# A cap on how far weight splitting runs ahead of the latent queries, and a later place for the squares of the queries' heads

## What is computed

```python
q  = (rms_norm(q_lat, q_a_gain) @ w_q_b).reshape(B, S, 8, 192)      # latent queries, 8 heads of 128 + 64 (rope)
kv = (rms_norm(kv_lat, kv_a_gain) @ w_kv_b).reshape(B, S, 8, 256)
q, k = rms_norm(q, q_gain), rms_norm(k, k_gain)                     # per head: needs the sum of squares of each head
q = concat([q[..., :128], rope(q[..., 128:], positions)])
p = softmax(q @ k.T * 192 ** -0.5)                                  # causal
o_mla = p @ v
mixed = concat([rms_norm(o_mla, g1), rms_norm(o_swa, g2)])
h = x + mixed @ w_out
```

## Time and profile before

| | |
|---|---|
| median of 3 runs | 3234.4 us (3231.15 to 3234.57) |
| the profiled execution: its own time | 3236.4 us |
| its span in the trace | 3234.6 us |
| TensorE (PE) busy | 99% |
| VectorE (DVE) busy | 65% |
| ScalarE (ACT) busy | 47% |
| mean DMA rate | 204 GB/s |
| weight splits: DVE L2140, ACT L1908 | 1101 each, 1223 and 1058 ns |

### The profile page before, as it was taken

One profiled execution on the slowest core, in us unless ns is written; L12 is line 12 of the kernel. 1 busy time (PEld: TensorE's weight loads), 2 busy tenths in 40 slices (PEclk: granted clock), 3 DMA queues, 4 the chain that ended last, 5 costly groups with the idle time before them and its releaser, 6 DMA issues.

```text
span 3234.6 us, 41995 instructions
## 1 busy us (share of the span) xinstructions
PE 3188.9 (99%) x16160; PEld 2708.1 (84%) x16160; DVE 2094.1 (65%) x3069; ACT 1524.5 (47%) x2006; POOL 526.6 (16%) x322
## 2 busy tenths in 40 slices
PE   9899999999999999999999999999999999999998
PEld 7788888888888888888888888888887888888886
DVE  6776688887555576666666665555465655555556
ACT  5645554445444444444444544455444544444443
POOL 0010007777777600000000000000000000000000
PEclk9999999999999999999999999999999999999999
DMA  6457558888888886677775555455655555555554
GB/s 220 150 198 265 173 194 212 212 212 214 213 214 212 229 304 230 242 247 242 248 245 195 188 193 175 161 172 173 202 197 179 178 193 193 189 192 193 189 191 148
DMA packets 220296, 661.04 MB, mean 204 GB/s; under 512 B 56704, under 2 KB 56848, under 8 KB 217536
## 3 DMA queue, kind: packets, MB, share of 16 engines
q1 hardware_dynamic: 170864, 600.81, 55.8%
q0 software_dynamic: 49232, 57.54, 8.4%
HBM read 622.48 MB, written 35.78 MB: 204 GB/s over the span
## 4 chain that ended last, share of the span: by engine, by line
PE 94%; DVE 4%; ACT 1%; issue 1%; DMA 0%; DVEq 0%; SPq 0%; ACTq 0%
PE PS L1676 93%; PE PS L1754 2%; DVE wlo L2140 1%; ACT whi L1908 0%; DVE R L2658 0%; DVE AA L2186 0%; DVE BB L2186 0%; DVE Y L2288 0%; ACT Y L1994 0%; DMA R<-in_x 0%; DVE M L2318 0%; DVE RT L2121 0%; DVE RT L2123 0%; DVE RT L2125 0%; ACT M L1892 0%
## 5 line engine op out<-in xcount | busy, mean ns | idle before, releaser
L2140 DVE TENSOR_TENSOR wlo<-raw,whi 128x1024 fp32r<-128x1024 f32 x1101 | 1342.6, 1223 | 732.8 <-ACT whi L1908 727.3
L1908 ACT ACTIVATE whi<-raw 128x1024 fp32r<-128x1024 f32 x1101 | 1159.1, 1058 | 1004.3 <-PE PS L1676 989.4
L1676 PE MATMUL PS<-whi,AA 128*128 128x512 f32 (+1 forms) x2880 | 716.9, 389 | 1.8 <-DVE AA L2186 1.2
L1676 PE MATMUL PS<-whi,BB 128*128 128x512 f32 x2640 | 666.7, 393 | 1.7 <-DVE wlo L2140 1.2
L1676 PEld LDWEIGHTS PS<-whi,AA 128*128 128x128 f32 x2880 | 535.8, 188 | 111.3 <-DVE AA L2186 2.0
L1676 PE MATMUL PS<-BB,whi 128*128 128x512 f32 x2304 | 577.4, 392 | 1.7 <-DVE BB L2186 1.7
L1676 PEld LDWEIGHTS PS<-whi,BB 128*128 128x128 f32 x2640 | 491.3, 188 | 102.2 <-DVE wlo L2140 1.6
L2751 POOL DMA_INDIRECT scr_g<-M x256 | 481.6, 1881 | 365.4 <-DVE M L2531 228.3
L1676 PEld LDWEIGHTS PS<-BB,whi 128*128 128x128 f32 x2304 | 414.4, 189 | 76.0 <-DVE BB L2186 1.9
L1676 PE MATMUL PS<-wlo,AA 128*128 128x512 f32 (+1 forms) x1440 | 388.3, 387 | 0.0
L1676 PE MATMUL PS<-wlo,BB 128*128 128x512 f32 x1320 | 356.4, 390 | 0.5 <-DVE wlo L2140 0.5
(11 more groups left out here) (239 smaller groups left out, 1480.7 us busy)
## 6 DMA issues: line engine op xcount, KB each, us to landing
raw<-in_peer_u SPq DMA_DIRECT2D x256, 512.0 KB, 4.1
raw<-in_peer_v SPq DMA_DIRECT2D x256, 512.0 KB, 4.2
raw<-in_w_in SPq DMA_DIRECT2D x160, 512.0 KB, 3.3
raw<-in_w_up SPq DMA_DIRECT2D x128, 512.0 KB, 4.1
raw<-in_w_down SPq DMA_DIRECT2D x128, 512.0 KB, 4.0
raw<-in_w_out SPq DMA_DIRECT2D x64, 512.0 KB, 4.3
raw<-in_w_in_a SPq DMA_DIRECT2D x32, 512.0 KB, 4.0
scr_g<-M POOLq DMA_DIRECT2D x8, 2048.0 KB, 33.3
```

The costliest lines, as they stand in the source:

```text
L1676: return e.matmul(outp, l, r, start=start, stop=stop)
L1908: e.activation(whi[:, n % NH, :], raw[:, n % NR, :], ACT.Copy).then_inc(s_hi, 1)
L2140: e.tensor_tensor(wlo[:, n % NH, :], raw[:, n % NR, :], bf(whi[:, n % NH, :]), ALU.subtract).then_inc(s_lo, 1)
```

## The change

Two things. While `queries(1)` and the side work behind it are emitted, `ensure_split` stops at the last piece of `w_q_b` (so neither the splits of w_out 0 and 1 nor the loads that go with them, of w_out 4 and 5, are emitted there); the cap is lifted when the attention begins, and the next call of `piece`, at the first product of `w_out`, emits what is missing. And `q_nope` emits its transposes and splits first, at its first step, and its squares only when all transposed blocks of queries and keys have been emitted.

```diff
             at, n_split, n_load = [0], [0], [0]
+            split_end = [len(order) - 1]
             low_held = []
...
             def ensure_split(i, hold=False):
-                while n_split[0] <= min(i, len(order) - 1):
+                while n_split[0] <= min(i, split_end[0]):
...
             def q_nope(ts, te, j):
+                while not a_free:
+                    yield
+                yield from trans_split(lambda kt, t: ts[:, t, 128 * kt:128 * kt + 128], 4, hl(AH, 4 * j), hl(AL, 4 * j),
+                                       lambda kt: GC[:, 88:89], te, a_free, qt_done)
+                turned = latest["PE"]
+                while len(qt_done) < 6 or len(kt_done) < 8:
+                    yield
                 for t in range(2):
                     t_ssq.append((yield from squares(heads(ts[:, t, :], 4), 4, ssq[:, 0, t, 4 * j:4 * j + 4], te)))
-                    yield
-                while not a_free:
-                    yield
-                yield from trans_split(lambda kt, t: ts[:, t, 128 * kt:128 * kt + 128], 4, hl(AH, 4 * j), hl(AL, 4 * j),
-                                       lambda kt: GC[:, 88:89], te, a_free, qt_done)
-                qrows.give(ts, t_ssq, latest["PE"])
+                qrows.give(ts, t_ssq, turned)
...
+            split_end[0] = order.index(("w_q_b", 3))
             queries(1)
             tasks.append(q_scale())
             tasks.append(pairs_freed())
             lend_banks()
             while len(qt_done) < 6 or len(kt_done) < 8 or not t_rq:
                 step()
+            split_end[0] = len(order) - 1
             idle.append(bias_gen())
```

More of the change, by code:

```diff
@@ L820, in q_nope @@
             def q_nope(ts, te, j):
-                for t in range(2):
-                    t_ssq.append((yield from squares(heads(ts[:, t, :], 4), 4, ssq[:, 0, t, 4 * j:4 * j + 4], te)))
-                    yield
                 while not a_free:
@@ L827, in q_nope @@
                                        lambda kt: GC[:, 88:89], te, a_free, qt_done)
-                qrows.give(ts, t_ssq, latest["PE"])
+                turned = latest["PE"]
+                while len(qt_done) < 6 or len(kt_done) < 8:
+                    yield
+                for t in range(2):
+                    t_ssq.append((yield from squares(heads(ts[:, t, :], 4), 4, ssq[:, 0, t, 4 * j:4 * j + 4], te)))
+                qrows.give(ts, t_ssq, turned)
             def q_rope(ts, te, j):
```

## The result

The changed kernel takes **3237.84 us** (median of 17 runs, 3236.43 to 3241.88); the kernel before takes 3233.88 (17 runs beside them, 3230.0 to 3234.57). The ratio is 1.0015 [1.0008, 1.0021]: about 4 us slower. That is less than the 0.2% which the prediction took for what can be told from no change, but the interval leaves out 1. The forecast was 3236.5.

A forecast was written before the change was run, and what follows sets the result against it. TensorE, busy 3188.9 of 3234.6 us, was taken as the bound. Terms +0.3, +2.5 and -0.7 gave +2.1 on the profiled 3236.4, so 3238.5, or 3236.5 on the median, which lies 2.0 lower; range 3234 to 3239.

The forecast's parts named there:

- The stall: At q_nope(0)'s first transposes, queued ahead of the last w_q_b pieces: TensorE waits 4.4 us for VectorE's evacuation.
- The clock behind it: After the stall TensorE's clock falls to half for 6.8 us, so the last w_q_b product ends at 153.5.
- VectorE's chain to the scores: From the last w_q_b product, evacuation, splits and rope spreading take 7.4 us; scores start at 160.9, +0.3 us.
- The scores: Forecast: half clock for 10.1 us as before; rival: full clock, up to 5 us faster, total 3232.5, chance 0.14.
- The late squares: Squares and scale before the first maximum hide behind half-clock scores: cost nothing, bounds 0 to 1 us.
- The start of `w_out`: First w_out products wait 2.2 us for the high split and 0.3 for the low: +2.5 us, unhidden.
- The long instruction: The 2.46 us TENSOR_SCALAR at 209.50 moves to about 212.0, near the end of GpSimd's issues: -0.7 us.
- my rival of 3235.9: At the long TENSOR_SCALAR, the port rule frees the whole 1.3 us; its chance is counted in the forecast's 0.50.
- the order does not bite: At q_nope(0)'s first step no bank is free, so no stall; scores at about 157, total 3232.6, chance 0.06.
- the stall lets the clock be: Full clock behind the stall at q_nope(0): scores at 158.0, 2.6 us earlier, total 3233.6, chance 0.14.
- the slower one: From the stall through w_out, each clock fall lasts 10.1 us instead of 6.8: total +6.4, 3240.8, chance 0.13.
- the signs of being wrong: No w_q_b gap; scores over 2 us off 160.9; no w_out wait; L2256 at 2.4 us; full clock at 144 to 150.

The follow-up runs named there:

- e3: Changed kernel, but q_nope(0) lets four steps of the walk pass before its first transposes: 3234.94 us, ratio 1.0006.
- e2: Kernel before with only the new order of q_nope, without the cap: 3232.75 us, ratio 1.0003.
- f1: Changed kernel with the negation in biased_max as SCALAR_TENSOR_TENSOR instead of TENSOR_SCALAR: 3237.21 us, ratio 1.0009.
- f4: Changed kernel with the splits of w_out 0 and 1 emitted right behind the scale of the queries: 3236.72 us, ratio 1.0009.
- e1: Kernel before with only the cap on the splits, q_nope as before: 3233.72 us, ratio 1.0000.
- f3: e4 with the negation in biased_max as SCALAR_TENSOR_TENSOR instead of TENSOR_SCALAR: 3227.7 us, ratio 0.9987.
- e4: e1 with the splits of w_out 0 and 1 emitted behind the scale of the queries, ahead of the first maxima: 3230.46 us, ratio 0.9992.
- f2: Kernel before with the negation in biased_max as SCALAR_TENSOR_TENSOR instead of TENSOR_SCALAR: 3230.95 us, ratio 0.9994.

## Why the prediction came out right, step by step

**The stall: right.** Forecast 4.4 us before transposes at 143.95, for want of VectorE's evacuation. Measured 4.2, at 144.84 on a trace that runs 0.8 us later. It stands in every kernel with the new order (4.21 or 4.22 us in five traces) except e3, which removes it by letting four steps pass.

**The clock behind it: a fall, but half as long.** Forecast 6.8 us at half; some 3.4 in both executions of the changed kernel and in e2, 6.7 in f1 and f4. So the last product of `w_q_b` ends at 152.8, which is 152.0 on the trace before, and not 153.5.

**VectorE's chain to the scores: 0.7 short.** Forecast 7.4 us; from 152.81 to 160.89 it is 8.1. The sum did not have two waits, 0.46 us for ScalarE at 154.02 and 0.63 for GpSimd's memset at 155.34; the instructions overlap by the rest. Scores at 160.89 on the trace are a start 0.5 us earlier than before, against +0.3 forecast: the fall that was 1.5 us too dear and the chain that was 0.7 too short work against each other.

**The scores: the rival came in halfway.** I had them at half clock for 10.1 us as before and gave full clock a chance of 0.14 and up to 5 us. They were at half for some 3.4. Without its wait of 2.0, `w_out` starts 37.5 us behind the scores, against 40.0 in the profiled execution before and 35.6 in its second. In f1 and f4 the scores run at full clock, as in the rival. What I did not consider is that the kernel before does both, so that this saving exists only against the execution that I read. The late squares, which I put at nothing with 0 to 1 us as bounds, cost TensorE no wait here, and 0.87 us in f1.

**The start of `w_out`: right.** Forecast 2.2 + 0.3; measured 1.96, and 0.44 of the weight load. In the two traces of the changed kernel no half clock follows this wait. In e1 and e3 one of some 3.4 us does, which the term of 2.5 us did not hold.

**The long instruction: the failed step.** I followed the second 128x4 TENSOR_SCALAR of the earlier trace rows (209.50), moved it to 212.0 near the end of GpSimd's issues and took a credit of 0.7. That one is indeed short now (211.82, 0.17 us). But the first, which took 0.17 us at 205.88 in the trace before, moved too, from 1.2 to 3.6 us behind the start of the issues, and is held in its place. TensorE waits 3.00 instead of 1.30, and the 3.5 us of half clock behind it (212.5 to 216, TensorE busy throughout) cost some 1.7 more, so the term is about +3.4 and not -0.7. I had moved one instruction of the two and forgotten the other. The Trainium skill ("SBUF — State Buffer", Who interferes with whom) has VectorE's 2-port forms and GpSimd block each other for a whole instruction; the traces agree in that the instruction is held up only within the issues and another form of it never is. They do not show what it is held until: GpSimd's single issues start 1.0 us apart (203.23, 204.27, 205.30), and it is held over several of them, to 7.26 us behind the start of the first. Used on the second instruction alone, as in my rival of 3235.9, it pointed the wrong way.

**The sum.** Up to the first attention the changed kernel is 2.3 us behind the profiled execution of before: -0.5 at the scores, -2.5 behind them, +2.0 for the wait at `w_out` and +3.4 from there on. The forecast was +2.1, from other parts: +0.3, 0, +2.5, -0.7. The agreement is thus partly luck. The medians differ by 4.0, which lies between the 2.3 against the first trace of before and the 6.7 against the second. Of the other rivals, "the order does not bite" and "the stall lets the clock be" fell with the stretches; the slower one (half clock everywhere for 10.1 us) did not happen, though its 3240.8 lies inside the runs' spread. Of the signs of being wrong one came, the long instruction with TensorE idle behind it, and one in part: the clock is back at 1.00 from 147.7 on.

**What stays open.** In the profiled execution of the changed kernel a further wait stands at 1146 us, where data come back from a scatter; in the second it does not.

```profile
1138.78 0.76 DVE L2564 TENSOR_TENSOR M<-M 128x256 f32<-128x256 f32 x2 [3.78 <-DMA M<-scr_g]
...
1145.99 2.14 PE L1681 MATMUL PS<-whi,AA 128*128 128x512 f32 x8 [2.67 <-DVE AA L2571]
```

In the second execution VectorE waited 0.53 us there, and in no other trace more than 0.9. This wait and what follows it are 3.3 us between the two ends of the changed kernel in the table. Whether the change makes it more frequent was not tried. Nor was it found what decides how long a stretch at half clock lasts and where it falls, so the cause of the 4 us is shown in its waits and not in its clock.

## What to carry to other kernels

Where several engines take turns, two edits that act in front of the same instruction do not add: the cap and the order alone cost nothing that can be measured and together cost 4 us. Before a split, a square or a load is moved into a gap, look at who else uses it: the splits gained 3.3 us in the gap ahead of the first maximum when it was empty, and about 1 us, not clear of the noise, when the squares were in it. And when a wait of 2 us is put ahead of a busy stretch, follow each later instruction of every engine against what runs beside it, the short ones too; f3 (the cap, splits in the scores and the other negation) is 0.13% faster than before, while the change as made is 0.15% slower.

## What the runs showed of the hardware

**A small instruction held until a fixed point.** While GpSimd issues its seven DMAs of 2 MB in 8.0 us, VectorE's 128x4 TENSOR_SCALAR either takes 0.17 us or is held until one of two points. In us from the start of the issues, each read from the trace's timeline of 196 to 216 us:

| kernel | issues start | first one begins, takes | second begins, takes | long one ends at |
|---|---|---|---|---|
| before, profiled | 204.70 | +1.18, 0.17 | +4.80, 2.46 | +7.26 |
| before, second | 200.42 | +1.53, 0.77 | +5.15, 2.10 | +2.30 and +7.25 |
| changed, profiled | 202.15 | +3.58, 3.68 | +9.67, 0.17 | +7.26 |
| changed, second | 201.44 | +3.56, 3.70 | +9.67, 0.17 | +7.26 |
| e1 | 199.43 | +5.12, 2.15 | +9.68, 0.17 | +7.27 |
| e2 | 201.96 | +1.42, 0.88 | +5.05, 2.21 | +2.30 and +7.26 |
| e3 | 197.14 | +5.03, 2.24 | +9.68, 0.17 | +7.27 |
| e4 | 199.37 | +1.12, 0.17 | +4.74, 2.52 | +7.26 |
| f4 | 206.14 | +1.65, 0.65 | +5.29, 1.97 | +2.30 and +7.26 |

When it is held, its price is the distance to that point, up to 3.7 us. Begun at +1.12 or +1.18, or behind the issues, it was not held; begun at +1.42 to +1.65 or +3.56 to +5.29 it was. SCALAR_TENSOR_TENSOR with two inputs of the same size took 0.16 to 0.17 us inside the issues in f1, f2 and f3.

**One kernel, two clocks.** The same instructions ran the scores at 0.50 for 10.1 us in one execution and at 1.00 in another, and `w_out` started 4.4 us apart. Behind the same stall of 4.2 us the clock stood at half for some 3.4 us in three traces and for 6.7 in two. For a change worth a few tenths of a per cent, one profiled execution of before is not enough to read the clock from.
